# One gathered edge tile in place of two partly filled gate tiles, in a 512-token transformer kernel

## What is computed

```python
u = rmsnorm(x, norm_g) @ w_in                 # 1024 -> 2 * 1536
xb, gate = u[..., :1536], u[..., 1536:]
xb = causal_depthwise_conv(xb, conv_w, conv_b)
xs = xb.reshape(bsz, seq, 16, 96)             # 16 blocks of 96 features
r = sigmoid(einsum('bshi,hij->bshj', xs, wr) + br)   # block-diagonal gates
i = sigmoid(einsum('bshi,hij->bshj', xs, wi) + bi)
log_a = -8.0 * r * softplus(-lam)
a = exp(log_a)
b = sqrt(-expm1(2.0 * log_a)) * (i * xb)
h = scan(a, b)                                # along the tokens
x = x + (h * silu(gate)) @ w_out
```

## Time and profile before

| what | us |
|---|---|
| median of 3 runs | 1308.51 (1307.96 to 1309.65) |
| the profiled execution's own time | 1308.73 |
| its span, first to last instruction | 1306.8 |
| TensorE busy (matmuls) | 1271.8 (97%) |
| TensorE weight loads busy | 942.5 (72%) |
| VectorE busy | 703.0 (54%) |
| ScalarE busy | 562.0 (43%) |
| GpSimd busy | 198.0 (15%) |

### The profile page before, as it was taken

The page is one execution under the profiler, slowest core; times in us unless marked ns, Lnnn a source line. Parts: engine busy times, 40 slices in busy tenths (PEclk is TensorE's granted clock), DMA queues, the critical chain, the costliest instruction groups (busy, mean ns, idle before and its releaser), DMA issues.

```text
span 1306.8 us, 15285 instructions
## 1 busy us (share of the span) xinstructions
PE 1271.8 (97%) x5362; PEld 942.5 (72%) x5362; DVE 703.0 (54%) x1293; ACT 562.0 (43%) x1098; POOL 198.0 (15%) x229
## 2 busy tenths in 40 slices
PE   5999999999999999999999999999999999999997
PEld 4778668777766677776765555788788888888885
DVE  6687787654557665465574444455544333444242
ACT  5557656532455544254443333333444322344231
POOL 1021022220222203032242231001100000000021
PEclk8999999999999999999999999999999999999998
DMA  5222313642111123221153221222332222332221
GB/s 183 87 74 95 100 65 97 184 141 66 48 34 48 33 71 97 91 73 57 57 131 77 53 71 49 81 97 81 97 97 91 89 95 97 97 97 91 89 79 65
DMA packets 45778, 111.88 MB, mean 86 GB/s; under 512 B 18127, under 2 KB 18375, under 8 KB 45703
## 3 DMA queue, kind: packets, MB, share of 16 engines
q1 hardware_dynamic: 42951, 104.09, 25.3%
q0 software_dynamic: 2320, 6.03, 2.2%
q10 hardware_dynamic: 432, 0.79, 0.2%
HBM read 102.76 MB, written 6.03 MB: 83 GB/s over the span
## 4 chain that ended last, share of the span: by engine, by line
PE 82%; issue 3%; DVE 3%; ACT 3%; POOL 1%; POOLq 0%; ACTq 0%; DVEq 0%
PE ps L580 23%; PE ps L581 22%; PE ps L582 21%; PE ps L709 3%; PE ps L739 2%; PE ps L732 2%; PE ps L678 2%; PE ps L735 2%; PE ps L686 1%; PE ps L697 1%; DVE xs L1140 1%; DVE cc L1172 1%; PE ps L696 1%; PE ps L644 1%; PE ps L627 1%
## 5 line engine op out<-in xcount | busy, mean ns | idle before, releaser
L1048 DVE TENSOR_TENSOR wl<-raw,wh 128x512 fp32r<-128x512 f32 x366 | 278.7, 767 | 206.3 <-ACT wh L766 128.8
L580 PE MATMUL ps<-xgh,wh 128*128 128x512 f32 x848 | 371.4, 438 | 15.1 <-ACT xgh L773 7.9
L581 PE MATMUL ps<-xgl,wh 128*128 128x512 f32 x848 | 337.9, 398 | 0.0
L582 PE MATMUL ps<-xgh,wl 128*128 128x512 f32 x848 | 335.5, 396 | 0.0
L766 ACT ACTIVATE wh<-raw 128x512 fp32r<-128x512 f32 x366 | 225.3, 623 | 191.4 <-PE ps L582 180.8
L580 PEld LDWEIGHTS ps<-xgh,wh 128*128 128x128 f32 x848 | 160.7, 189 | 99.7 <-issue 64.7
L582 PEld LDWEIGHTS ps<-xgh,wl 128*128 128x128 f32 x848 | 160.2, 189 | 39.3
L581 PEld LDWEIGHTS ps<-xgl,wh 128*128 128x128 f32 x848 | 161.0, 190 | 32.4 <-issue 2.4
L1546 POOL TENSOR_SCALAR Pt<-Pt,stat 128x256 f32<-128x256 f32 (+3 forms) x128 | 80.3, 639 | 339.7 <-DVE stat L1306 255.0
L929 ACT ACTIVATE Pt<-Pt,stat 128x256 f32<-128x256 f32 (+3 forms) x128 | 71.7, 560 | 134.1 <-DVE stat L1274 58.6
L581 PE MATMUL ps<-fl,wh 128*128 128x512 f32 x256 | 102.1, 399 | 0.0
(11 more groups left out here) (222 smaller groups left out, 1756.6 us busy)
## 6 DMA issues: line engine op xcount, KB each, us to landing
raw<-wst SPq DMA_DIRECT2D x183, 512.0 KB, 3.4
skew<-rps POOLq DMA_DIRECT2D x1, 3840.0 KB, 30.1
bst<-skew SPq DMA_DIRECT2D x16, 224.0 KB, 4.6
xt<-xT SPq DMA_DIRECT2D x3, 512.0 KB, 7.0
outT<-ot SPq DMA_DIRECT2D x6, 256.0 KB, 2.2
kb<-ybh POOLq DMA_DIRECT2D x8, 128.0 KB, 2.4
cstt<-cst SPq DMA_DIRECT2D x1, 551.5 KB, 9.3
ybh<-ybh POOLq DMA_DIRECT2D x4, 128.0 KB, 2.5
```

The costliest lines, as they stand in the source:

```text
L580: e.matmul(o, high, a, start=(k == 0), stop=False)
L581: e.matmul(o, high, b, start=False, stop=False)
L582: e.matmul(o, low, a, start=False, stop=stop).then_inc(tile_done, 1)
L1048: e.tensor_tensor(wl_t[:, i, :], raw_t[:, u % NRAW, h % 2 * 512:h % 2 * 512 + 512], f32(wh_t[:, i, :]), ALU.subtract).then_inc(lo_done, 1)
```

## The change

`GATE_TILES` loses (0, 1) and (2, 1), the middle chunk's two tiles that hold 32 useful rows each, and gains one tile (3, 1) with both. Its weights have rows 0 to 31 from the third chunk's block, rows 96 to 127 from the first chunk's, and zeros between. Its input is a new pair of tiles, `halo_h` and `halo_l`, whose rows 0 to 31 and 96 to 127 are copied from `xsh_t` and `xsl_t` by DMAs that POOL issues: two when the first chunk of a group is split, two when the third is (64 KB each), and for group 0 two more that fill rows 32 to 95 once with finite values. The pair lies where `sq[0]` and `sq[1]` lie. A group has 60 tiles in place of 62, the stream 1456 in place of 1464. The plain numbers of the later ticks become the same offsets from `A_END`, `B_END` and `C_END`.

```diff
-GATE_TILES = [(0, 0), (1, 0), (0, 1), (1, 1), (2, 1), (1, 2), (2, 2)]
+GATE_TILES = [(0, 0), (1, 0), (1, 1), (3, 1), (1, 2), (2, 2)]
...
+        ph = ExitStack()
+        halo_h, halo_l = sb("halo_h", [128, S], R, ph)[:, :], sb("halo_l", [128, S], R, ph)[:, :]
+        ph.close()
...
-        SETS = {"s": (0, 16, 406.0, 0.655), "w": (16, 24, 602.0, 1.22), "n": (24, 32, 697.0, 1.12)}
+        SETS = {"s": (0, 16, A_END + 62.0, 0.655), "w": (16, 24, B_END + 50.0, 1.22),
+                "n": (24, 32, B_END + 145.0, 1.12)}
...
-        NORM_AT = [13.5, 347.5, 555.5, 955.5, 4000.0]
+        NORM_AT = [13.5, A_END + 3.5, B_END + 3.5, C_END + 3.5, 4000.0]
...
                     ks = [a for a, m in GATE_TILES if m == name[1] % 3]
+                    if ks[k] == 3:
+                        q.wait_ge(halo_in, 32 + 64 * (name[1] // 3 + 1))
+                        return halo_h, halo_l
...
+            def halo(g):
+
+                yield ev_at["conv", 3 * g] + 6.5
+                q.wait_ge(xsh_done, 3 * g + 1)
+                q.wait_ge(xsl_done, 3 * g + 1)
+                if g:
+                    q.wait_ge(tile_done, end["gi", 3 * g - 2] + 1)
+                else:
+                    q.wait_ge(sum_done, 4)
+                    q.wait_ge(odd_done, 4)
+                    e.dma_start(halo_h[32:96, :], xsh_t[32:96, 0, :]).then_inc(halo_in, 16)
+                    e.dma_start(halo_l[32:96, :], xsl_t[32:96, 0, :]).then_inc(halo_in, 16)
+                e.dma_start(halo_h[96:128, :], xsh_t[96:128, 3 * g % 4, :]).then_inc(halo_in, 16)
+                e.dma_start(halo_l[96:128, :], xsl_t[96:128, 3 * g % 4, :]).then_inc(halo_in, 16)
+                yield ev_at["conv", 3 * g + 2] + 6.5
+                q.wait_ge(xsh_done, 3 * g + 3)
+                q.wait_ge(xsl_done, 3 * g + 3)
+                e.dma_start(halo_h[0:32, :], xsh_t[0:32, (3 * g + 2) % 4, :]).then_inc(halo_in, 16)
+                e.dma_start(halo_l[0:32, :], xsl_t[0:32, (3 * g + 2) % 4, :]).then_inc(halo_in, 16)
...
-                    if m_ == m:
+                    if m_ == m and k < 3:
                         add(gw[g, 128 * k:128 * k + 128, 128 * m:128 * m + 128][None])
+                    elif m_ == m:
+                        edge = np.zeros((128, 128), np.float32)
+                        edge[:32] = gw[g, 256:288, 128:256]
+                        edge[96:] = gw[g, 96:128, 128:256]
+                        add(edge[None])
```

More of the change, by code:

```diff
@@ L270, in build @@
         x_in = [sem(f"x_in{i}") for i in range(5)]
-        par_in, cst_in, sel_in, rp_in, skew_in = (sem(n) for n in ("par_in", "cst_in", "sel_in", "rp_in", "skew_in"))
+        halo_in, par_in, cst_in, sel_in, rp_in, skew_in = (sem(n) for n in ("halo_in", "par_in", "cst_in", "sel_in", "rp_in", "skew_in"))
         bias_in = [sem(f"bias_in{i}") for i in range(2)]
@@ L1579, in _ @@
             lanes = [zeros(), first_sums(), skews(), masks(), finals()] + [sums(s) for s in (1, 2, 3, 4)]
-            lanes += [inputs(g) for g in range(4)] + [y_low(c) for c in range(12)] + [normals(kind) for kind in SETS]
+            lanes += [lane(g) for g in range(4) for lane in (halo, inputs)] + [y_low(c) for c in range(12)] + [normals(kind) for kind in SETS]
             lanes += [lane(c) for c in range(4) for lane in (move_kb, move_qb)]
```

## The result

The changed kernel takes 1313.92 us in the median of 6 runs (1312.31 to 1315.45), where the kernel before takes 1308.51: a ratio of 1.0042, 95% interval 1.0029 to 1.0055. The forecast was 1313.5. The profiled execution took 1312.8 us, with a span of 1311.0, 4.2 us more than before.

The account below looks back on a forecast made before the run. The prediction took the chain of ScalarE and VectorE to bound the first layer, not TensorE. Terms + 4.56, + 1.46 and - 1.04 sum to + 4.98: 1308.73 becomes 1313.7, median 0.22 lower, 1313.5; range 1307.0 to 1316.5.

Parts of the forecast that it names:

- What bounds the stage: First layer: the chain of ScalarE and VectorE sets the time, so TensorE's 5.6 us saved count nothing and return as waits.
- the tile in `wa`: Tile after the first layer's groups: start moves from 229.25 to 234.2, set by the chain; TensorE could start it at 231.6.
- Order: First layer's turns: 60 tiles a group give remainder 0 modulo 4 every time, the old order behind group 1; main term.
- Roots to first scan: Part of each turn: 4.39 us in all three, where it was 2.11, 4.39, 2.11; + 4.56 us.
- the silu stage: Last part of each turn: 8.17 us in all three, where it was 7.44, 8.17, 7.44; + 1.46 us.
- the gates stage: From first gate eviction to roots: groups 0 and 2 lose one high split of 0.52 us each; - 1.04 us.
- The sum: The terms over the first layer's turns together: + 4.98 us.
- Gathered rows: The 18 DMAs on POOL's list: landing in 2.4 us, in time for the edge tile, taken at 0.
- the upper bounds, 9.6 and 7.0: Most the DMAs could cost: 4 landings of 2.4 us wholly exposed, or 12 issues of 0.58 us slowing VectorE.
- TensorE as the bound: Rival: TensorE, 97% busy, is the bound after all, so 5.6 us are saved, 1302.9; chance 0.08.
- the long turn was chance: Rival: group 1's 48.7 us turn is not the order's; only two gates-stage splits are saved, 1307.5; chance 0.12.
- Gathering: Rival: POOL's 12 issues lock VectorE out for their full length, 7.0 us on top, 1320.5; chance 0.08.

Follow-up runs that it names:

- experiment 4: Changed kernel with weight splits 20 to 31 and 50 to 60 two ticks earlier, as before the change behind groups 0 and 2: 1309.1 us, ratio 1.0003.
- experiment 1: Changed kernel with weight splits 12 to 60, high and low parts alike, two ticks earlier: 1307.04 us, ratio 0.9987.
- experiment 5: Changed kernel with weight splits 12 to 69 two ticks earlier, so including the stretch behind the last group: 1303.55 us, ratio 0.9954.
- experiment 3: Kernel before, 62 tiles, with the change's 18 DMAs issued into tiles that no matmul reads: 1308.74 us, ratio 1.0.
- experiment 7: Changed kernel without its 18 DMAs, the edge tile reading the third chunk's own rows (middle chunks' gates not right): 1315.57 us, ratio 1.0041.
- experiment 6: Kernel before, nothing gathered, with weight splits 36 to 46 two ticks earlier, in its one long turn: 1306.36 us, ratio 0.998.
- experiment 8: Changed kernel with weight splits 12 to 69 one tick earlier: 1304.6 us, ratio 0.9966.
- experiment 2: Kernel before, nothing gathered, with weight splits 12 to 59 two ticks earlier: 1310.24 us, ratio 1.001.

## Why the prediction was right, point by point

- **What bounds the stage.** Right. From group 0's first gate eviction to 233 us ScalarE and VectorE waited for TensorE in one place of the changed kernel, 0.3 us at group 0's gates, and the eight tiles' 5.6 us came back as waits: 16.6 us where I had said about 18. TensorE was ready for the tile in `wa` at 231.15 (said 231.6). I had expected single waits below 2 us; this one is 2.34, and the granted clock is 1.00 all the same. Experiment 4 shows the bound apart from the order.
- **Order.** Right in each term. Roots to first scan is 4.39, 4.40, 4.41 (said 4.39), the silu stage 8.17 three times (said 8.17), first scan to first silu eviction 23.93, 23.91, 23.91, the gates stage 12.61, 12.22, 12.21, 12.21 (said one split of 0.52 less in groups 0 and 2).
- **The sum.** From first gate eviction to the tile in `wa` it was 170.18 us and is 175.06: + 4.88 for + 4.98. The span grew by 4.2 because this execution reached group 0's gates 0.64 earlier. Over all ten traces that mark lies between 57.48 and 61.06, and two kernels that are the same up to there (experiments 1 and 5) have 59.71 and 61.06. So the chain's + 4.98 is confirmed to 0.1 us, but that the median came within 0.4 us of the forecast (+ 5.4 in place of + 5.0) is in part luck. The range was looser than its terms: with issues at 0.1 each the forecast's upper end is 1314.7, not 1315.5, and nothing stands for the way up to 1316.5.
- **Gathered rows.** Taken at 0, and 0 it is (experiments 3 and 7). My landing time was too low for one transfer in four, 4.0 us where I took 2.4; the margin of 3.5 held it. The 1.2 us that I left in the range for VectorE beside an issue did not show in the turns of experiment 3, and the upper bounds, 9.6 and 7.0, were far off.
- **The rivals.** TensorE as the bound is out: experiment 4 stands at 1.0003 where it asked for 0.996. That the long turn was chance is out: it was made and unmade by the ticks alone in six kernels. Gathering is out.
- **What I didn't see.** The prediction treated the order as given. The same sum says that the order is worth more than the change, and it could have said so: three turns of the short kind, 3 x 3.01 us less. Experiment 1 is that, and experiment 5 adds the stretch behind group 3. The prediction also didn't see how near TensorE was behind the bound: at the tile in `wa` the two arrived together, and once the chain is shorter TensorE takes over there. And the expectation for experiment 1 left out the clock: it was right for the chain and 2 us low for the whole.

What the change is worth with the order right in both: the second and third turn are 45.7 with it (experiment 5) and 46.2 without (experiment 6), 0.5 us each, one split that ScalarE no longer makes in the gates stage. The first is 46.7 without it, since group 0's gates hold, beside that split, ScalarE's wait for TensorE (0.27). The whole times are 1303.55 and 1306.36. In the two traces the turns make 2.0 us between them and the stretch behind group 3 makes 3.7 (75.24 against 78.91), while experiment 5's execution reached group 0's gates 3.6 later. Those 3.7 are the order that only experiment 5 mended, the tiles and the low clock in experiment 6 together; the runs don't tell these apart.

## What to carry to other kernels

An engine that is 97% busy is not the bound of a stage if nobody waits for it there: ask of each other engine where it waits for the busy one, and if it is nowhere, work taken from the busy one is worth nothing as long as the others are as slow as they are. Then look how close behind it is: here, with the order of the splits mended, the busy engine became the bound again at the end of the layer, and tiles taken from it there should count; no run tested that. Where a schedule is laid out by a period (a split every four tiles) and the work repeats with another (62 tiles), the remainder decides who stands in front of whom; taking two tiles away changed it for groups 0 and 2 and cost about as much, 5.4 us, as the tiles could at best have brought, 5.6. Before such a change, cut the repeated stage into its parts and compare the repetitions with each other: the kernel before already held both orders side by side, and their difference was the forecast.

## What the runs showed of the hardware

- Single stretches of about 3.4 us at half the granted clock (1.2 in place of 2.4 GHz) came up between 36 and 1290 us in five of the ten traces, eight in all, and in places that changed from run to run: in the third turn at 182 to 184 us (experiments 1, 6 and 8), in the second at 138.5 (experiment 5), at or just behind the norm after `wa` (experiments 1, 3 and 5) and near 934 us (experiment 1). The kernels before and after and experiments 2, 4 and 7 had none there. Each began within about 2.2 us behind the end of a wait of TensorE of 0.9 to 2.1 us, as many other waits end that no such stretch follows: what calls them up is open. From the norm after `wa` to the last norm it is 1014.6 to 1015.0 us in the seven traces without one in between, 1016.3 and 1016.4 with one, and 1018.0 with two, so one costs about 1.5 us where TensorE is the bound. In the turns it cost nothing (45.66 and 45.69 against 45.7); in experiment 6 the stretch behind group 3 came out 1.0 us longer.
- An issue of a DMA on POOL took 0.5 to 0.6 us (the first one 0.74), and two-input operations of VectorE beside it were no longer (experiment 3). POOL's own tensor operations can lengthen them: a scan takes 1.22 us alone, 2.31 where it begins while one of POOL's products runs (119.73 in experiment 1, the products from 118.40 to 123.13). The Trainium skill (SBUF — State Buffer, "SBUF: two separate sides") has two-input operations of VectorE in conflict only with a GpSimd operation that reads SBUF, and issues locked out by VectorE's two-port modes, which none of these operations is shown to use here. The runs agree with the first; on the second they show nothing.
- SBUF to SBUF copies of 64 KB from 32 partitions landed in 1.9 and 2.1 us (medians of the changed kernel), and four of its 16 in 4.0.
